# Moving the modulation's first sixteen weight units behind later chunks of w_in, and one bank and the mean's place in na_in

## The chip, the cores and the metric

One core of one Trainium2 chip runs one program. The metric is the device time of one execution in microseconds (us); lower is better. The kernel before takes 1294.21 us, the median of 3 runs (1294.12 to 1294.3).

## What is computed

Two blocks over 256 tokens of width 1024, in float32. The first is an RMS norm, one wide projection w_in (pooling input, q, k, v, index q and k, index weights, gates), pooling and an indexed sparse attention, an output projection, and a convolutional feed-forward. The second is modulated by a vector `ada`, made from two condition vectors and a weight of 2 x 1024 x 6144, and has a mixer, a neighbourhood attention over 16 heads, and feed-forwards. What matters here, cut from the reference:

```
proj = xn @ w_in
score = einsum('bqh,bhqk->bqk', w, relu(einsum('bqhd,bkd->bhqk', iqb, ik) * 64**-0.5))
_, idx = lax.top_k(score, 64)
o = softmax over the chosen keys, times v
...
sx1, cx1, gx1, sx2, cx2, gx2 = split(silu(c) @ ada_w[i] + ada_b[i])
sc1, cc1, gc1, sc2, cc2, gc2 = split(silu(c_ctx) @ ada_w[i] + ada_b[i])
hx = _modulate(_rms(x, g), sx1, cx1)
...
q, k, v = _heads(hx, w_q, q_g), _heads(hx, w_k, k_g), _heads(hx, w_v)   # q and k normed per head
```

## The kernel before, in words

All weights come as **units** of 128 x 1024 float32 (512 KB). `PLAN` (`weight_plan`, line 105) is one list of all units in the order in which they are loaded. SyncE (SP) loads unit i into `raw[i % 9]` (`load`, line 517) as soon as TensorE (PE) is done with unit i - 9; it waits for that in the order of the list, so a ring of nine buffers runs ahead of PE. ScalarE (ACT) makes the high part of a unit, `whi` (L1401, four buffers), and VectorE (DVE) the low part, `wlo`, in place of `raw` (L1917). PE multiplies each 128 x 128 block three times (L634, L646, L648), so a chunk of w_in (one unit, eight blocks) is 24 matmuls of 128 x 256. Which `hi` and `lo` an engine makes at which step is a table of `split_places` (line 153): ACT copies a unit three to four chunks ahead of PE, and waits there for the unit's load (L1399). Each engine takes its instructions in program order, so what stands behind such a copy on ACT waits with it.

w_in's 37 chunks carry other work between them. PE does an index step behind chunks 11 to 18 (`index_heads`, L915; ACT's relu L1464; DVE sums, then finds the largest at L2082 and L2084 behind chunks 16 to 23). Behind chunks 25, 27, 29 and 31 PE makes the attention's scores (`scores1`, L927). DVE masks them and finds the maxima (L2101, L2104), ACT takes the exponential (`exp1`, L1472), DVE the inverses (L2112), GpSimd (POOL) the probabilities (L2729). PE turns those behind chunks 27 to 34 (`turned1`, L936), and ACT copies them out (`copied1`, L1479), which PE waits for before it turns the next head in the same bank and before `values1` (L948) behind chunks 29, 31, 33 and 35. DVE evicts each chunk (`rescaled_in`, L1944).

`ada`'s first sixteen units, called ada 0 to 15, are multiplied on PE (`ada_unit`, L802) into bank 7, in four **runs** of four behind w_in's chunks 9, 13, 17 and 21 (`ADA_AFTER`). DVE copies the bank once, behind the last run (L1951), and PE turns it behind chunk 34. The other 80 units are summed on DVE and are not touched here.

na_in has 24 chunks (`NA_CHUNKS`: k0 q0 v0 k1 q1 k2 ...), a k or v chunk 128 x 512, a q chunk 128 x 256. A chunk's bank is its place in the list of all chunks modulo 3, unless `APART` names one; `bank_free` (line 728) holds PE until the bank is read. For k and q, ACT copies and squares the product (L1841, L1844), PE sums the squares (L1218), DVE takes the mean (`mean_of`, L2503), ACT and POOL make the root, DVE scales (L2509). `scores2` (L1225) uses the same two banks, 4 and 5, in turn with these sums: a use waits until the last but one is read (`na_bank`). Bank 3 is otherwise used by `product2` (L1252) for the values.

Of the kernel before, what the change touches and what calls it, by code (L numbers as in the profile page):

```python
# [46 lines left out]
ADA_STEPS = 96  # L47

LOW_P = range(2)
ADA_AFTER = {"w_in": (6, 16)}  # L50

# [44 lines left out]
             "w_down": "down_r", "ab_in": "ab", "ab_out": "about_r", "w1_0a": "r0a", "w2_0a": "d0a_r",  # L98
             "w1_0b": "r0b", "w2_0b": "d0b_r", "na_in": "na", "na_out": "nao_r", "w1_1": "r1", "w2_1": "d1_r"}

APART = {("w_in", 3): 3, ("w_in", 4): 5, ("w_in", 5): 7, ("pool_w", 1): 5, ("pool_w", 3): 4, ("na_out", 3): 4, ("na_out", 4): 5, ("na_out", 5): 7}
NRAW, NHI = 9, 4


def weight_plan():


    plan, following, order = [], {}, []
    taken, added = [n for n in range(ADA_STEPS) if n not in MOD], MOD[:]

    def modulation(count, places, units):
        for _ in range(count):
            places.append(len(plan))
            plan.append(("ada", units.pop(0)))

    for name in ORDER:
        kt, nt = WEIGHTS[name]
        first, upto = ADA_AFTER.get(name, (0, 0))
        for u in range(-(-kt * nt // 8)):
            order.append(len(plan))  # L120
            plan.append((name, u))
            here = following[name, u] = []
            if u > first and (u - first) % 4 == 3 and upto and taken:
                modulation(4, here, taken)
            modulation(sum(x == u for x in MOD_AFTER.get(name, ())), here, added)
            order += here
    assert not taken and not added and sorted(order) == list(range(len(plan)))
    return plan, following, order


PLAN, FOLLOWING, TAKEN = weight_plan()
TAKEN_AT = {i: e for e, i in enumerate(TAKEN)}
UNIT = {key: i for i, key in enumerate(PLAN)}
# [5 lines left out]
def walk(name):  # L139

    kt, nt = WEIGHTS[name]
    for blk in range(kt * nt):
        if blk % 8 == 0:
            yield "unit", blk // 8
        if blk % kt == kt - 1:
            yield "chunk", blk // kt
        if blk % 8 == 7 or blk == kt * nt - 1:
            yield "after", blk // 8
            for i in FOLLOWING[name, blk // 8]:
                yield "ada", i  # L150
# [124 lines left out]
def bank_left(name, n):  # L275

    if n < EARLY.get(name, 0):
        return "resc_" + name, n + 1
    if name == "ab_in" and n >= 8:
        return "ab_v", n - 7  # L280
    if (name, n) == ("ab_out", 6):
        return "about_r", 15
    twice = name in ("ab_out", "w2_0a", "w2_0b")
    return BANK_READ[name], 2 * n + 2 if twice else n + 1


def launch_program(nc, dram, out):
# [5 lines left out]
    S = Signals(nc)  # L293
# [54 lines left out]
    def param(name, i=0, n=1):  # L348
        at, _ = PARAMS[name]
        return par[:, at + i:at + i + n]  # L350
# [23 lines left out]
    def bank_of(name, n):  # L374
        return ps[APART.get((name, n), CHUNK_AT[name, n] % 3)]

# [56 lines left out]
    def rows_of(h):  # L433
        return slice(64 * (h % 2), 64 * (h % 2) + 64)
# [21 lines left out]
    scores_after = {START2[p] + b: (p, b) for p in range(8) for b in range(2)}  # L456
# [9 lines left out]
    def norm2(n):  # L466

        kind, c = NA_CHUNKS[n] if 0 <= n < 24 else ("v", 0)
        if kind == "v":
            return None  # L470
        return (2 * c, k2[c % 3], 512) if kind == "k" else (2 * c + 1, q2[c % 3], 256)
# [119 lines left out]
    def tensor_program(e):  # L591
        w = Waits(e)
        bank6 = [None]

        def linear(name, T, acts, hi_ready, lo_ready, during=None, following=None, midway=None, begin=0,
# [5 lines left out]
            for n in range(begin, upto or nt):  # L601
                Tn = T(n) if callable(T) else T
                g = CHUNK_AT[name, n]
                bank = bank_of(name, n)
                o = bank[:, :Tn]
                bank_free(name, n)
                for k in range(kt):
                    blk = n * kt + k
# [119 lines left out]
        def bank_free(name, n):  # L728

            if name == "na_out" and n in (3, 4):  # L730
                w.wait_ge(S("na_bank"), len(turn2))
            elif name == "na_out" and n == 5:
                w.wait_ge(S("p2_pt1"), 16)
            elif name == "na_out" and n >= 6:
                w.wait_ge(S("nao_r"), n - 5)
            elif name == "pool_w" and n in (1, 3):
                w.wait_ge(S("sc_x"), 8)
            elif (name, n) == ("w_attn", 0):

                w.wait_ge(S("resc_w_in"), 36)  # L740
            elif name == "w_in" and n < 9:

                if n >= 6:
                    w.wait_ge(S("resc_w_in"), n - 5)
            elif CHUNK_AT[name, n] >= 3:
                signal, count = bank_left(*CHUNKS[CHUNK_AT[name, n] - 3])
                w.wait_ge(S(signal), count)
# [495 lines left out]
        def product2(p):  # L1243

            w.wait_ge(S("p2_pt0"), 2 * p + 2)
            w.wait_ge(S("p2_pt1"), 2 * p + 2)
            w.wait_ge(S("v2"), p + 1)
            if p:
                w.wait_ge(S("o2"), p)
            for k in range(4):  # L1250
                for x in range(2):
                    m = e.matmul(ps[3][rows_of(x), 0:256], v2[p % 3][:, k, rows_of(x)], pts[x][:, 256 * k:256 * k + 256],  # L1252
                                 start=k == 0, stop=k == 3)
            m.then_inc(S("pv2").sem, 1)
# [17 lines left out]
        def after_na(u):  # L1272
            turned, scores, values = attend2(u)
            if values is not None:
                product2(values)
            if turned:
                turned2(*turned)
            if scores:
                scores2(*scores)
# [628 lines left out]
    def vector_program(e):  # L1908
        w = Waits(e)
# [10 lines left out]
        def los(i):  # L1920
            for s in LO_AT[i]:
                lo(s)
# [79 lines left out]
        def written(name, n):  # L2002
            if (name, n) in MOD_SUMMED:
                ada_copied(MOD_SUMMED[name, n])
            if (name, n) in ADA_WRITTEN:
                ada_out(ADA_WRITTEN[name, n])
# [301 lines left out]
        for what, i in walk("ab_in"):  # L2308
            if what == "unit":
                los(UNIT["ab_in", i])  # L2310
            if what == "chunk":
                n, c = i, i % 4
# [133 lines left out]
        for x in "ab":  # L2446
            name, down = "w1_0" + x, "w2_0" + x
# [50 lines left out]
        def head_mean(j, T):  # L2498
            w.wait_ge(S("hn_sum"), j + 1)
            if j >= 2:  # L2500
                w.wait_ge(S("hn_rr"), j - 1)
            bank = ps[4 + turn2["norm", j] % 2]
            e.tensor_scalar(tmp[j % 2][:, :T], bank[:, :T], 1.0 / 64, EPS, MUL, ADD).then_inc(S("na_bank").sem, 1)  # L2503

        def head_out(j, T, dst, gain):
            c, kind = j // 2, j % 2
            w.wait_ge(S("hn_rr"), j + 1)
            w.wait_ge(S("na_copy"), j + 1)
            e.scalar_tensor_tensor(dst, dst, gain, tmp[2 + j % 2][:, :T], MUL, MUL).then_inc(S("hn_out").sem, 1)  # L2509

        def values_out(c):
            w.wait_ge(S("v2_tr"), c + 1)
            if c >= 3:
                w.wait_ge(S("pv2"), c - 2)
            e.tensor_copy(v2[c % 3], ps[6].rearrange("p (t c) -> p t c", t=4)).then_inc(S("v2").sem, 1)
# [36 lines left out]
        def after_na(u):  # L2552
            turned, scores, values = attend2(u)
            if values is not None:
                out2(values)
            if turned:
                turned2(*turned)
            if u == 24:
                lo(SPLIT_AT["na_out", 2])
            if scores:  # L2560
                scores2(*scores)
            if u == 24:
                lo(SPLIT_AT["na_out", 3])

        def values_before(n):

            if n and not norm2(n - 1):
                values_out(NA_CHUNKS[n - 1][1])

        def mean_of(n):  # L2570
            if norm2(n):
                j, _, T = norm2(n)
                head_mean(j, T)

        def during_na(n):

            if n > 4:
                mean_of(n - 1)
            for m in () if n == 2 else (0, 1) if n == 3 else (n - 2,):
                if norm2(m):  # L2580
                    j, dst, T = norm2(m)
                    head_out(j, T, dst, param("q_g" if j % 2 else "k_g"))
            if n < 4:
                mean_of(n - 1)
            written("na_in", n)

        for what, i in walk("na_in"):
            if what == "unit":
                if i not in (3, 4):
                    values_before(i)  # L2590
                if i == 4:
                    mean_of(3)
                if i:
                    los(UNIT["na_in", i])
                if i == 4:
                    values_before(3)
            if what == "chunk":
                during_na(i)
            if what == "after":
                after_na(i)  # L2600
# [18 lines left out]
        for what, i in walk("w1_1"):  # L2619
            if what == "unit":  # L2620
                los(UNIT["w1_1", i])
            if what == "chunk":
                n = i
# [379 lines left out]
```

## Time and profile before

| | |
|---|---|
| median of 3 runs | 1294.21 us |
| the profiled execution's own time | 1294.86 us |
| its span, first to last instruction | 1293.1 us |
| PE busy | 1275.7 us |
| DVE, ACT, POOL busy | 964.6, 594.9, 424.9 us |
| granted TensorE clock, mean | 1.00 |
| read from HBM | 217.21 MB |

The span is all but 1.8 us of the execution's own time. Busy times are sums of the instructions' spans; the ends of matmuls are modelled, so a stall of PE is best seen as the distance between the starts of two matmuls. The page gives the share of the span for each engine; w_in runs from 7 to about 147 us, na_in from 899 to about 1092 us.

### The profile page before, as it was taken

The numbers are of one execution on the slowest core, as the hardware profiler recorded it, in microseconds if no ns is written. First come the engines' busy times: TensorE is split into PE (matmuls) and PEld (weight loads), VectorE is DVE, ScalarE is ACT, GpSimd is POOL, SyncE is SP. The second block draws the span as 40 slices with busy tenths as digits, with TensorE's granted clock in tenths as the row PEclk, the third lists the DMA queues.
The fourth block names the chain that finished last, engine by engine and source line by source line (L and its number), as shares of the span: only waits on it lengthen the run. The fifth ranks groups of instructions, "written<-read, shape, count | busy, mean of one in ns | idle before, by whom it ended". The sixth has DMA issues, their size and how long they took to land.

```text
span 1293.1 us, 19800 instructions
## 1 busy us (share of the span) xinstructions
PE 1275.7 (99%) x7680; PEld 1097.0 (85%) x7680; DVE 964.6 (75%) x1380; ACT 594.9 (46%) x968; POOL 424.9 (33%) x416
## 2 busy tenths in 40 slices
PE   8999999999999999999999999999999999999999
PEld 8888989999888888888788787888767777998887
DVE  6688698999987898897667476566677766977553
ACT  6237556666653233444211243223555554766432
POOL 1562131333330002365200266012466552454100
PEclk9999999999999999999999999999999999999999
DMA  9774466555663553354456365563232332555552
GB/s 306 264 262 157 151 211 199 181 180 186 205 214 112 188 207 126 115 170 159 148 194 194 116 226 210 189 228 127 107 107 73 115 98 70 183 187 186 190 182 79
DMA packets 66268, 219.96 MB, mean 170 GB/s; under 512 B 9120, under 2 KB 12448, under 8 KB 66176
## 3 DMA queue, kind: packets, MB, share of 16 engines
q1 hardware_dynamic: 65888, 218.46, 50.3%
q8 instruction: 61, 1.00, 0.3%
q10 hardware_dynamic: 288, 0.25, 0.1%
q14 instruction: 31, 0.25, 0.1%
HBM read 217.21 MB, written 1.05 MB: 169 GB/s over the span
## 4 chain that ended last, share of the span: by engine, by line
PE 75%; DVE 14%; issue 5%; DMA 2%; ACT 2%; POOL 1%; SPq 0%; DVEq 0%; ACTq 0%; POOLq 0%
PE ps L634 15%; PE ps L648 15%; PE ps L646 15%; PE ps L624 11%; PE ps L626 6%; DVE wlo L1917 4%; DVE tmp L2207 2%; DMA raw<-in_w_in 2%; DVE Y L1944 1%; PE ps L1225 1%; PE ps L1252 1%; PE ps L1239 1%; DVE modsum L1999 1%; PE ps L1218 1%; PE ps L718 1%
## 5 line engine op out<-in xcount | busy, mean ns | idle before, releaser
L1401 ACT ACTIVATE whi<-raw 128x1024 fp32r<-128x1024 f32 (+1 forms) x302 | 317.3, 1052 | 305.5 <-DMA raw<-in_w_0b 73.7
L634 PE MATMUL ps<-A,whi 128*128 128x256 f32 (+2 forms) x1332 | 440.4, 331 | 0.8 <-ACT sq L1844 0.8
L1917 DVE TENSOR_TENSOR wlo<-raw,whi 128x1024 fp32r<-128x1024 f32 (+1 forms) x302 | 400.8, 1332 | 47.7 <-ACT whi L1401 47.7
L648 PE MATMUL ps<-A,wlo 128*128 128x256 f32 (+2 forms) x1312 | 422.9, 322 | 1.7 <-DVE wlo L1917 1.7
L646 PE MATMUL ps<-A,whi 128*128 128x256 f32 (+2 forms) x1312 | 422.4, 322 | 0.2 <-DVE A L1930 0.2
L634 PEld LDWEIGHTS ps<-A,whi 128*128 128x128 f32 x1332 | 253.0, 190 | 41.6 <-issue 18.5
L648 PEld LDWEIGHTS ps<-A,wlo 128*128 128x128 f32 x1312 | 249.2, 190 | 21.8 <-DVE wlo L1917 2.5
L646 PEld LDWEIGHTS ps<-A,whi 128*128 128x128 f32 x1312 | 249.4, 190 | 20.2 <-issue 1.7
L1999 DVE SCALAR_TENSOR_TENSOR modsum<-raw,cond,modsum 128x1024 f32<-128x1024 f32 x98 | 154.4, 1605 | 0.0
L624 PE MATMUL ps<-H,whi 128*128 128x512 f32 x400 | 141.8, 399 | 0.2 <-POOL H L2672 0.2
L2672 POOL TENSOR_TENSOR H<-tmp,H 128x256 fp32r<-128x256 f32 (+1 forms) x86 | 111.9, 1301 | 88.7 <-ACT H L1736 75.1
L626 PE MATMUL ps<-H,wlo 128*128 128x256 f32 x400 | 112.5, 281 | 0.5 <-DVE wlo L1917 0.4
L2808 POOL TENSOR_TENSOR tmp<-tmp 128x512 f32<-128x512 f32 (+1 forms) x42 | 60.7, 1445 | 132.8 <-ACT tmp L1728 132.8
L648 PE MATMUL ps<-H,wlo 128*128 128x512 f32 (+1 forms) x264 | 100.3, 380 | 0.6 <-DVE wlo L1917 0.6
L634 PE MATMUL ps<-H,whi 128*128 128x512 f32 (+1 forms) x264 | 100.4, 380 | 0.0
L646 PE MATMUL ps<-H,whi 128*128 128x512 f32 (+1 forms) x264 | 100.2, 379 | 0.0
L624 PEld LDWEIGHTS ps<-H,whi 128*128 128x128 f32 x400 | 75.2, 188 | 18.9 <-issue 0.5
L2683 POOL TENSOR_TENSOR ssum<-ssum,sq 128x256 f32<-128x256 f32 (+1 forms) x29 | 33.3, 1149 | 161.7 <-ACT sq L1420 161.7
L626 PEld LDWEIGHTS ps<-H,wlo 128*128 128x128 f32 x400 | 75.6, 189 | 1.2 <-DVE wlo L1917 1.2
L624 PE MATMUL ps<-A,whi 128*128 128x512 f32 x182 | 65.2, 394 | 0.0
L2359 DVE SCALAR_TENSOR_TENSOR R<-ps,ada,R 128x256 f32<-128x256 f32 x50 | 22.2, 478 | 52.3 <-PE ps L648 51.8
L648 PEld LDWEIGHTS ps<-H,wlo 128*128 128x128 f32 x264 | 49.7, 188 | 10.1 <-DVE wlo L1917 0.8
(369 smaller groups left out, 1846.5 us busy)
## 6 DMA issues: line engine op xcount, KB each, us to landing
raw<-in_ada SPq DMA_DIRECT2D x96, 512.0 KB, 4.0
raw<-in_w SPq DMA_DIRECT2D x64, 512.0 KB, 3.5
raw<-in_w_up SPq DMA_DIRECT2D x44, 512.0 KB, 3.5
raw<-in_w_in SPq DMA_DIRECT2D x34, 512.0 KB, 5.9
raw<-in_w_0a SPq DMA_DIRECT2D x32, 512.0 KB, 3.8
raw<-in_w_0b SPq DMA_DIRECT2D x32, 512.0 KB, 3.6
raw<-in_na_in SPq DMA_DIRECT2D x24, 512.0 KB, 4.9
raw<-in_w_down SPq DMA_DIRECT2D x22, 512.0 KB, 3.5
```

Source lines behind the costliest of these rows:

```text
L624: e.matmul(bank, w_hi, both(k), start=k == 0, stop=False)
L626: m = e.matmul(o, w_lo, ah, start=False, stop=last)
L634: e.matmul(o, w_hi, ah, start=k == 0, stop=False)
L646: e.matmul(o, w_hi, al, start=False, stop=False)
L648: m = e.matmul(o, w_lo, ah, start=False, stop=last)
L1401: e.activation(whi[s % NHI][:, :cols], raw[i % NRAW][:, :cols], ACT.Copy).then_inc(S("whi").sem, 1)
L1917: e.tensor_tensor(wlo[i % NRAW][:, :cols], raw[i % NRAW][:, :cols], plain(whi[s % NHI][:, :cols]), SUB).then_inc(S("wlo").sem, 1)
L1999: d = e.scalar_tensor_tensor(total, raw[i % NRAW], cond[:, k, v:v + 1], total, MUL, ADD)
L2207: e.scalar_tensor_tensor(x[:, 1:256], o[:, 0:255], param("conv_w", 44 + ch), x[:, 1:256], MUL, ADD).then_inc(own.sem, own.up())
L2672: e.tensor_tensor(into, x, plain(hi), SUB).then_inc(S(done).sem, 1)
L2683: e.tensor_tensor(total, total, x, ADD).then_inc(S(st + "_part").sem, 1)
L2808: e.tensor_tensor(x, x, x, MUL).then_inc(S(st + "_sq").sem, 1)
```

## The change

`ADA_AFTER` now lists the chunks themselves: ada 0 to 3 stand behind chunk 25, ada 4 to 7 behind 27, 8 to 11 behind 29, 12 to 15 behind 31, each run after the attention's steps of that chunk. The plan of loads and the places of `hi` and `lo` follow. In na_in, chunk 3 goes to bank 3 in place of the bank of chunk 0, and waits for the last reader of bank 3 in w2_0b (`d0b_r`); the first `product2` waits for chunk 3's reader. On DVE the mean of chunk i - 1 stands ahead of the `lo` of unit i, not behind it, for nine i (those after a `scores2` step whose chunk i - 1 is a k or q); it stood so for i = 4 before.

```
-ADA_AFTER = {"w_in": (6, 16)}
+ADA_AFTER = {"w_in": (25, 27, 29, 31)}
...
-APART = {..., ("pool_w", 3): 4, ("na_out", 3): 4, ...}
+APART = {..., ("pool_w", 3): 4, ("na_in", 3): 3, ("na_out", 3): 4, ...}
...
-        first, upto = ADA_AFTER.get(name, (0, 0))
...
-            if u > first and (u - first) % 4 == 3 and upto and taken:
+            if u in ADA_AFTER.get(name, ()):
                 modulation(4, here, taken)
...
             if name == "na_out" and n in (3, 4):
                 w.wait_ge(S("na_bank"), len(turn2))
+            elif (name, n) == ("na_in", 3):
+                w.wait_ge(S("d0b_r"), 16)
...
             if p:
                 w.wait_ge(S("o2"), p)
+            else:
+                w.wait_ge(S("na"), 4)
...
+        MEAN_FIRST = [4, *(u + 1 for u in scores_after if 4 < u + 1 < 24)]
...
-            if n > 4:
+            if n > 4 and n not in MEAN_FIRST:
                 mean_of(n - 1)
...
-                if i == 4:
-                    mean_of(3)
+                if i in MEAN_FIRST:
+                    mean_of(i - 1)
                 if i:
                     los(UNIT["na_in", i])
```

SP's queue of loads, at w_in's chunks 26 to 31 before. The tiles raw_49 to raw_57 are the ring's nine buffers, in_w_in a chunk of w_in, in_ada a unit of ada:

```order
L530 DMA raw_55<-in_w_in 128x1024
L530 DMA raw_56<-in_w_in 128x1024
L530 DMA raw_57<-in_w_in 128x1024
L530 DMA raw_49<-in_w_in 128x1024
L530 DMA raw_50<-in_w_in 128x1024
L530 DMA raw_51<-in_w_in 128x1024
```

and now, from ada 4 to chunk 31 (the lines of the file have moved by one; chunks 26 and 27 stand just ahead):

```order
L529 DMA raw_54<-in_ada 128x1024
L529 DMA raw_55<-in_ada 128x1024
L529 DMA raw_56<-in_ada 128x1024
L529 DMA raw_57<-in_ada 128x1024
L529 DMA raw_49<-in_w_in 128x1024
L529 DMA raw_50<-in_w_in 128x1024
L529 DMA raw_51<-in_ada 128x1024
L529 DMA raw_52<-in_ada 128x1024
L529 DMA raw_53<-in_ada 128x1024
L529 DMA raw_54<-in_ada 128x1024
L529 DMA raw_55<-in_w_in 128x1024
L529 DMA raw_56<-in_w_in 128x1024
```

Each pair of chunks now has four units of ada ahead of it. The load of chunk 28 (raw_49) is the ring's ninth behind ada 1, that of chunk 29 behind ada 2, and those of chunks 30 and 31 behind ada 5 and 6.

ACT, from the copy of chunk 29 to the copy-out of the first turned head, before (whi_68 to whi_70 are copies of units; the ACT_TABLE_LOAD and the X tiles are the exponential; Y_102 is the copy-out):

```order
L1401 ACTIVATE whi_68<-raw_49 128x1024
L1472 ACT_TABLE_LOAD
L1472 ACTIVATE X_98,small<-X_98,small 128x128
L1472 ACTIVATE X_98,small<-X_98,small 128x256
L1472 ACTIVATE X_99,small<-X_99,small 128x128
L1472 ACTIVATE X_99,small<-X_99,small 128x256
L1527 ACTIVATE sig<-tmp_89 128x256
L1401 ACTIVATE whi_69<-raw_50 128x1024
L1527 ACTIVATE sig<-tmp_90 128x256
L1401 ACTIVATE whi_70<-raw_51 128x1024
L1479 ACTIVATE Y_102<-ps 128x384
```

and now, from the copy of chunk 28:

```order
L1404 ACTIVATE whi_67<-raw_49 128x1024
L1404 ACTIVATE whi_68<-raw_50 128x1024
L1475 ACT_TABLE_LOAD
L1475 ACTIVATE X_98,small<-X_98,small 128x128
L1475 ACTIVATE X_98,small<-X_98,small 128x256
L1475 ACTIVATE X_99,small<-X_99,small 128x128
L1475 ACTIVATE X_99,small<-X_99,small 128x256
L1530 ACTIVATE sig<-tmp_89 128x256
L1530 ACTIVATE sig<-tmp_90 128x256
L1404 ACTIVATE whi_69<-raw_55 128x1024
L1404 ACTIVATE whi_70<-raw_56 128x1024
L1482 ACTIVATE Y_102<-ps 128x384
```

As before, the copies of chunks 28 and 29 stand ahead of the first exponential, and those of 30 and 31 ahead of the first copy-out; what has moved is their place by a step or so, and the buffers that they read, which are those of the loads above. Chunks 32 and 33 stand in the same way ahead of the third head's copy-out.

DVE in na_in, at the step of unit 5, before (wlo_63 is the low part of a later unit, tmp_88 the mean for q1, k_1_145 a scaled k):

```order
L2531 TENSOR_REDUCE small<-X_99 128x1
L2536 RECIPROCAL small<-small 128x1 x2
L1917 TENSOR_TENSOR wlo_63<-raw_54,whi_70 128x1024
L2503 TENSOR_SCALAR tmp_88<-ps 128x256
L2509 SCALAR_TENSOR_TENSOR k_1_145<-k_1_145,par,tmp_89 128x512
```

and now:

```order
L2534 TENSOR_REDUCE small<-X_99 128x1
L2539 RECIPROCAL small<-small 128x1 x2
L2506 TENSOR_SCALAR tmp_88<-ps 128x256
L1920 TENSOR_TENSOR wlo_63<-raw_54,whi_70 128x1024
L2512 SCALAR_TENSOR_TENSOR k_1_145<-k_1_145,par,tmp_89 128x512
```

The mean has changed places with one low part; the other eight places read alike.

## Rows read from the trace of the kernel before

**Rows 1.** page, busy time of each engine over the span

```profile
PE 1275.7 (99%) x7680; PEld 1097.0 (85%) x7680; DVE 964.6 (75%) x1380; ACT 594.9 (46%) x968; POOL 424.9 (33%) x416
```

**Rows 2.** who PE waited for: us in total, times, longest us

```profile
PE ps L915 <- ACT tmp L1464: 1.8, 2, 1.2
...
PE ps L936 <- POOL Y L2729: 0.9, 1, 0.9
...
PE ps L634 <- ACT sq L1844: 0.8, 1, 0.8
...
PE ps L1225 <- DVE tmp L2503: 0.6, 1, 0.6
```

**Rows 3.** timeline of PE in w_in: start us, us, instruction, idle before and releaser

```profile
39.22 1.92 PE L802 MATMUL ps<-raw,cond 128*32 128x512 f32 x16
...
51.79 0.56 PE L915 MATMUL ps<-ik,iq 64*128 64x128 f32 x4 [1.24 <-ACT tmp L1464]
...
103.81 0.38 PE L634 MATMUL ps<-A,whi 128*128 128x256 f32 x1
...
110.81 0.55 PE L936 MATMUL ps<-con,Y 128*128 128x128 f32 x3 [0.93 <-POOL Y L2729]
...
128.94 0.39 PE L634 MATMUL ps<-A,whi 128*128 128x256 f32 x1
```

**Rows 4.** timeline of SP's DMA issues in w_in, around the first modulation run

```profile
40.31 1.28 SPq L530 DMA_DIRECT2D raw<-in_ada  x3
41.63 0.43 SPq L530 DMA_DIRECT2D raw<-in_w_in  x1
```

**Rows 5.** raw tiles' landing, issued in 40:41.4, 56:58.1, 73.2:75.8, 107:112

```profile
DMA to landing us min/median/max: 4.9/6.3/7.5
...
DMA to landing us min/median/max: 5.7/6.6/8.0
...
DMA to landing us min/median/max: 4.4/5.3/6.1
...
DMA to landing us min/median/max: 3.3/3.4/3.5
```

**Rows 6.** DMA issues by line in 41.5:42: count, KB each, median us to landing

```profile
raw<-in_w_in SPq DMA_DIRECT2D x1, 512.0 KB, 8.8
```

**Rows 7.** timeline of ACT in w_in

```profile
50.42 1.06 ACT L1401 ACTIVATE whi<-raw 128x1024 fp32r<-128x1024 f32 x1 [8.80 <-DMA raw<-in_w_in]
...
106.20 1.04 ACT L1401 ACTIVATE whi<-raw 128x1024 fp32r<-128x1024 f32 x1
107.26 1.28 ACT L1472 ACT_TABLE_LOAD   x1
```

**Rows 8.** timeline of DVE in w_in

```profile
68.43 1.23 DVE L1917 TENSOR_TENSOR wlo<-raw,whi 128x1024 fp32r<-128x1024 f32 x1 [2.75 <-ACT whi L1401]
69.58 0.41 DVE L1944 TENSOR_TENSOR vT<-ps,rst 128x256 f32<-128x256 f32 x1
...
94.96 0.68 DVE L1951 COPY tmp<-ps 128x512 f32<-128x512 f32 x1
...
96.69 0.42 DVE L1944 TENSOR_TENSOR tmp<-ps,rst 128x256 f32<-128x256 f32 x1
```

**Rows 9.** 80 to 96 us: length, PE, PEld, DVE, ACT, POOL (instructions), PEclk, DMA, GB/s

```profile
80.00:96.00 16.00, 16.00 (x135) 14.43 (x134) 15.27 (x39) 4.88 (x7) 14.64 (x20) 1.00 0.78 271
```

**Rows 10.** timeline of PE at the start of na_in

```profile
915.83 0.50 PE L634 MATMUL ps<-A,whi 128*128 128x512 f32 x1 [0.82 <-ACT sq L1844]
...
937.60 1.12 PE L1225 MATMUL ps<-k,q 64*128 64x512 f32 x2
...
939.31 0.69 PE L1225 MATMUL ps<-k,q 64*128 64x512 f32 x1 [0.59 <-DVE tmp L2503]
```

**Rows 11.** timeline of DVE at the start of na_in

```profile
937.15 1.77 DVE L1917 TENSOR_TENSOR wlo<-raw,whi 128x1024 fp32r<-128x1024 f32 x1
938.85 0.41 DVE L2503 TENSOR_SCALAR tmp<-ps 128x256 f32<-128x256 f32 x1
```

More of the change, by code:

```diff
@@ L99 @@
              "w1_0b": "r0b", "w2_0b": "d0b_r", "na_in": "na", "na_out": "nao_r", "w1_1": "r1", "w2_1": "d1_r"}
-APART = {("w_in", 3): 3, ("w_in", 4): 5, ("w_in", 5): 7, ("pool_w", 1): 5, ("pool_w", 3): 4, ("na_out", 3): 4, ("na_out", 4): 5, ("na_out", 5): 7}
+APART = {("w_in", 3): 3, ("w_in", 4): 5, ("w_in", 5): 7, ("pool_w", 1): 5, ("pool_w", 3): 4, ("na_in", 3): 3, ("na_out", 3): 4, ("na_out", 4): 5, ("na_out", 5): 7}
 NRAW, NHI = 9, 4
```

## The prediction, made before the changed kernel ran

> **What bounds the kernel now.** First the page's busy times: PE is busy for 1275.7 of 1293.1 us [rows 1], so what remains to gain are stalls of a microsecond or less, and any wait that is added to PE shows in full. Then the list of who PE waited for: in w_in it is ACT's relu (1.8 us in two stalls) and POOL's probabilities (0.9 us), in na_in the square that frees a bank (0.8 us) and the mean that frees bank 4 or 5 (0.6 us) [rows 2]. The timelines show what stands behind these. In w_in ACT sat idle for 8.80 us until 50.42, waiting for the load of chunk 14, and the relu that PE needed stood behind that copy [rows 7]; PE stalled for 1.24 us [rows 3]. The reader should see in this that a late load does not stop PE by itself. It stops ACT's queue, and PE meets it at the next thing that it needs from ACT. From 68.43 DVE does not pause until chunk 26 [rows 8]; it is 95% busy from 80 to 96 us, while PE still runs 135 matmuls in 16 us [rows 9], 0.12 us each or 2.9 us a chunk.
>
> **How loads land around a run.** This carries the forecast. A run of four units takes PE 1.9 us [rows 3]. As it frees four raw buffers, SP issues four loads, at 1.1, 1.5, 2.0 and 2.4 us after the run's start at 39.22 (40.31 to 41.63) [rows 4]. They landed 4.9, 6.3, 7.5 and 8.8 us after issue [rows 5, 6], so the third is there 9.5 us after the run's start, and the fourth 11.2. Reckoned alike with the medians and maxima of the two later bursts [rows 5], the third came at 10.0 and 8.1 us. A load alone takes 3.4 us [rows 5]. The moved runs make the same bursts. What differs is who waits. Before, the fourth load of a burst was chunk 14, copied by ACT some three chunks later. Now chunks 28 and 29 are the second and third loads of the first run's burst, 30 and 31 those of the second's, 32 and 33 those of the third's, and ACT's copies of them stand ahead of the exponential, and then ahead of the copy-out, that PE needs one or two chunks after the run. I take 9.3 us for the third load where one was issued just before the run, and 8.7 to 9 where not.
>
> **Step 1, chunks 9 to 25.** The four runs leave this stretch (7.5 us of PE), and with them the lateness of loads: chunk i's load now waits for chunk i - 9, which is 26 us of work ahead. Chunk 9 ends at 39.1 as before. Chunks 10 to 16 then take 7 x 2.9 and five index steps of about 0.5 [rows 3], to 62.3 us. DVE's unbroken stretch begins there: it evicts chunk 16 at 62.5 in place of 69.58 [rows 8]. The work between that and chunk 22's eviction is unchanged, but for the copy of bank 7 (0.6 us) [rows 8], so that comes at 89.0 in place of 96.69. PE loses most of its lead here, as it can start a chunk only when DVE has reached the eviction two chunks before (the low part stands just ahead of it): I count 2.1, 0.9, 0.5 and 0.5 us of waits for `wlo` at chunks 22 to 25. Chunk 25 ends at 95.0, scores take 0.9, and the first run ends at 97.9. Chunk 26 starts at 97.9 in place of 103.81 [rows 3]: **5.9 us earlier**, with three runs still to come. Bounds: 4 if DVE's steps are stretched by POOL in the new alignment, 7.5 if not at all limited by DVE.
>
> **Step 2, the three later runs: 3 x 1.9 = 5.6 us** on PE. Their own loads were issued long before, so nothing is added there.
>
> **Step 3, new waits of PE.** First run, start 96.0: chunk 29 lands at 105.3, its copy ends at 106.3. From the end of that copy (107.24) to the first turned head it took 3.6 us before, through table load, exponential, inverses and probabilities [rows 3, 7]; so PE can turn at 109.9. It is there after chunk 27, at 103.7: a stall of 6.2 us, where it was 1.0 before. Second run, start 111.2: chunk 31 lands at 119.9, copied at 121.0, the copy-out behind it takes 0.5; PE wants to turn the next head behind chunk 28 at 116.1: 5.4 us. Third run, start 126.9: chunk 33 at 135.9, copy, one more copy of 0.3, copy-out, 137.6; PE is there at 131.8: 5.8 us. Behind chunk 31 the copy of chunk 34 (the fourth load) costs 0.5 more. Sum 17.9, less the 1.0 of before: **+16.9**. The fourth run does no harm: the loads that it frees are for later stages. The queue behind the waiting copy holds all of ACT's work, and DVE's inverses and the evictions behind them; they get late by the same amount, and nothing of this is added to PE's stall. Bounds for the three stalls: with every load landing in 3.4 us they are 2.3, 2.1 and 2.4; with the third as late as the latest fourth (11.6) they are 8.5, 8.3 and 8.4.
>
> So w_in: -5.9 + 5.6 + 16.9 = +16.6 us. Behind it the engines wait for each other as before, PE most of all, and no load is near its limit, so I let the delay through to the end.
>
> **Step 4, na_in.** Chunk 3 no longer waits for chunk 0's square: -0.8 us [rows 10]. What is late next is the chain from the sum behind chunk 3's first half to the scores, which PE starts itself and which moves with it, so I keep the whole 0.8. The mean at unit 5: DVE made the low part from 937.15 to 938.92 and then the mean, PE's second scores matmul came at 939.31 where it could have followed the first of 937.60 after 0.5 [rows 10, 11]. With the mean first that wait is covered: -1.2. The low part is 0.4 later and has two chunks of lead. The other eight swaps have no wait of PE against them: nothing. **-2.0**, bounds -0.5 (both waits reappear at the next step) and -2.5.
>
> **Sum.** +16.6 - 2.0 = +14.6 on the profiled execution's 1294.86, so 1309.5; the median of the runs lies 0.65 lower, which gives 1308.8. I say 1308.5 us.
>
> **A rule against the change.** The granted clock is at its upper level, 2.4 GHz, in the row of 80 to 96 us [rows 9], and so it is in every other stretch; no wait of PE before is above 1.3 us, so no row shows what happens behind one of 5 or 6. The Trainium skill (TensorE: Matmul & The Clock Gate, The HAM clock gate) says that an idle PE falls back to 1.2 GHz and is given 2.4 again only when it has been busy; by it the new stalls would cost up to a chunk's 2.9 us again each, and the sum would be up to 1317. On loads the skill (DMA: Bandwidth & Descriptors, Anatomy of one DMA) puts a transfer at some 2.0 us and its bytes at 436 GB/s, 3.2 us for one load, near the 3.4 measured; its estimate for a third load in a row is 5.6 us, where the trace has 7.5, and by it the sum would be some 6 us lower. I go by the trace.
>
> **Rivals.**
> 1. The loads come quicker than in the three bursts, since the new ones are issued while PE's stalls leave DMA idle. The stalls are then between 2.2 and 4.5 us each, and the time is 1298 to 1304. For it: the third burst before was quicker by 1.4 us than the first. Against: a burst's third load is behind two others issued 0.45 us apart, whatever stands before.
> 2. PE comes back slower from each stall: 1313 to 1318. For it: three idle gaps far longer than any now. Against: part of a slower chunk 28 or 30 would be hidden in the next stall.
> 3. The other side: chunks 28 to 33 are in time, and only the gains stay. Then w_in gives -5.9 + 5.6 - 1.0 = -1.3, with na_in 1291. It decides at the landing: the third load would have to be there 3.3 us after the run's start, or have its buffer from another unit. It is issued 2.0 us after the start and takes 3.3 us at the least [rows 5], so only a fault in my reading of the ring brings this.
> 4. The two edits in na_in do nothing, because the waits move to the next step: 1310.5.
>
> **How the numbers follow.** The forecast and its neighbours within 4 us, rival 4 among them, 0.54; rival 1 0.18; rival 2 0.19; rival 3 0.07, and 0.02 for a time near that of before by a mixture. Left out on the two sides are the slowest part of rival 2 and the quickest of rival 1, beside rival 3: the range is 1299 to 1317. A measurement of this kernel can tell about 0.2% (2.6 us) from no change: faster 0.07, within 0.02, slower 0.91.
>
> **What would show it.** ACT should wait for in_w_in loads three times, ending near 105, 120 and 136, for 5 us and more. PE should wait at L936's successor for POOL's probabilities once (6 us) and for ACT's copy-out twice (5 to 6 us each). No wait of ACT for w_in between 36 and 95, no stall of PE at L915, some at L648 for `wlo` near 80 to 92. The first chunk behind the run at 96 should start near 98, the one behind the fourth near 145. In na_in chunk 3 should follow without a gap, and the mean stand right behind the inverses at unit 5. I am wrong if ACT's longest wait for a load in w_in is below 3 us, if PE has no stall above 3 us there, or if the clock falls.

## The result, and the profile after

The changed kernel takes 1313.09 us, the median of 4 runs (1311.96 to 1314.29); the kernel before, beside it, took 1294.26. The ratio is 1.0146, with an interval of 1.0134 to 1.0158. The forecast was 1308.5 with a range of 1299 to 1317. The profiled execution took 1311.96 us, its span is 1310.1.

The page's busy times after, against [rows 1]:

```profile
PE 1280.8 (98%) x7680; PEld 1101.6 (84%) x7680; DVE 969.9 (74%) x1380; ACT 594.7 (45%) x968; POOL 418.3 (32%) x416
```

The same 7680 matmuls keep PE busy 5.1 us longer. So the 17.0 us of span are not all waiting: some matmuls have become slower. Who PE waited for, against [rows 2] (us in total, times, longest):

```profile
PE ps L937 <- ACT Y L1482: 8.3, 2, 4.3
PE ps L647 <- DVE wlo L1920: 4.8, 7, 1.7
PE ps L937 <- POOL Y L2734: 4.8, 1, 4.8
```

The three stalls of the forecast are there, one for POOL and two for ACT's copy-out. The waits for the index steps, for the square that freed a bank and for the mean are gone from this view. The timeline of PE in w_in, against [rows 3]:

```profile
96.49 1.92 PE L803 MATMUL ps<-raw,cond 128*32 128x512 f32 x16
98.34 0.38 PE L633 MATMUL ps<-A,whi 128*128 128x256 f32 x1
...
109.14 0.90 PE L937 MATMUL ps<-con,Y 128*128 128x128 f32 x3 [4.79 <-POOL Y L2734]
...
121.45 0.87 PE L937 MATMUL ps<-con,Y 128*128 128x128 f32 x3 [4.03 <-ACT Y L1482]
...
122.34 0.41 PE L645 MATMUL ps<-A,whi 128*128 128x256 f32 x1
122.55 0.41 PE L647 MATMUL ps<-A,wlo 128*128 128x256 f32 x1
122.76 0.41 PE L633 MATMUL ps<-A,whi 128*128 128x256 f32 x1
...
138.66 0.88 PE L937 MATMUL ps<-con,Y 128*128 128x128 f32 x3 [4.30 <-ACT Y L1482]
...
148.39 0.38 PE L633 MATMUL ps<-A,whi 128*128 128x256 f32 x1
```

Chunk 26 starts at 98.34, 5.47 us earlier than before, and chunk 32 at 148.39, 19.45 us later. Behind 121.45 matmuls of 128x256 stand 0.21 us apart, where it was 0.12. ACT's timeline says what the stalls are made of:

```profile
103.26 1.06 ACT L1404 ACTIVATE whi<-raw 128x1024 fp32r<-128x1024 f32 x1 [5.42 <-DMA raw<-in_w_in]
104.52 1.06 ACT L1404 ACTIVATE whi<-raw 128x1024 fp32r<-128x1024 f32 x1 [0.21 <-DMA raw<-in_w_in]
105.60 1.28 ACT L1475 ACT_TABLE_LOAD   x1
...
118.60 1.06 ACT L1404 ACTIVATE whi<-raw 128x1024 fp32r<-128x1024 f32 x1 [8.53 <-DMA raw<-in_w_in]
...
135.57 1.06 ACT L1404 ACTIVATE whi<-raw 128x1024 fp32r<-128x1024 f32 x1 [7.27 <-DMA raw<-in_w_in]
```

Three waits for loads of w_in, of 5.4, 8.5 and 7.3 us, each with a second copy 1.2 us behind it. From the end of the second copy at 105.58 to the first turned head at 109.14 it takes 3.56 us, as it did before (3.6). The windows give the clock (length, then PE, PEld, DVE, ACT, POOL, then PEclk, DMA share, GB/s):

```profile
105.00:106.00 1.00, 0.00 (x0) 0.00 (x0) 0.57 (x1) 0.98 (x2) 0.00 (x0) 1.00 1.04 397
106.00:107.00 1.00, 0.00 (x0) 0.00 (x0) 0.00 (x0) 0.99 (x2) 0.00 (x0) 0.78 1.01 365
107.00:108.00 1.00, 0.00 (x0) 0.00 (x0) 0.09 (x1) 1.00 (x5) 0.00 (x0) 0.50 0.40 160
112.00:113.00 1.00, 1.00 (x8) 0.20 (x4) 0.96 (x4) 0.00 (x0) 0.00 (x0) 0.50 0.00 0
113.00:114.00 1.00, 1.00 (x12) 0.19 (x4) 0.97 (x4) 0.00 (x0) 0.00 (x0) 0.81 0.00 0
114.00:115.00 1.00, 1.00 (x10) 0.71 (x7) 1.00 (x1) 0.00 (x0) 0.00 (x0) 1.00 0.51 123
```

PE stops at 104.3. The granted clock goes from 2.4 to 1.2 GHz at about 106.5, while PE is idle; PE works again from 109.14, and the clock is back shortly after 113. The same happens behind the other two stalls. That agrees with the rule of the Trainium skill cited in the prediction (TensorE: Matmul & The Clock Gate, The HAM clock gate). No stretch of the kernel before could show it: its longest wait of PE is 1.24 us.

In na_in the timeline of PE, against [rows 10]:

```profile
955.60 1.13 PE L1226 MATMUL ps<-k,q 64*128 64x512 f32 x4
958.85 1.10 PE L1219 MATMUL ps<-sq,con 128*128 128x512 f32 x2 [0.49 <-DVE X L2532]
```

The four scores matmuls run in one piece. A new wait of 0.49 us for DVE has come behind them, at the next sum of squares. The two kernels lie 19.07 us apart just ahead of na_in (the norm's matmuls there start at 896.38 and 915.45), 18.00 at the first sum of squares (918.69 and 936.69) and 17.04 at the first matmul behind the sum at 958.85 (942.34 and 959.38): the edits gave 2.03 us.

### The profile page after: what moved, and what is told of

Same layout as the page of the kernel before. It is cut to its first block, busy times and chain, and to the rows that moved or that the text cites. A ratio compares the mean times of both kernels' runs of the same rounds, so it can differ in the third digit from the quotient of the medians.

```text
span 1310.1 us, 19800 instructions
## 1 busy us (share of the span) xinstructions
PE 1280.8 (98%) x7680; PEld 1101.6 (84%) x7680; DVE 969.9 (74%) x1380; ACT 594.7 (45%) x968; POOL 418.3 (32%) x416
## 4 chain that ended last, share of the span: by engine, by line
PE 75%; DVE 15%; issue 5%; ACT 2%; DMA 2%; POOL 1%; SPq 0%; DVEq 0%; ACTq 0%; POOLq 0%
PE ps L633 15%; PE ps L647 15%; PE ps L645 15%; PE ps L623 11%; PE ps L625 5%; DVE wlo L1920 5%; DVE tmp L2210 2%; DMA raw<-in_w_in 2%; DVE Y L1947 1%; PE ps L1255 1%; PE ps L1226 1%; PE ps L1240 1%; DVE modsum L2002 1%; DVE score L2069 1%; PE ps L803 1%
```

## The experiments

The theory after this reading: a run of four frees its buffers late, the load of a chunk then lands behind the time at which ACT wants to copy it, and what PE needs stands in ACT's queue behind that copy. The fall of the clock comes on top. Rivals: the loads themselves bind PE, whatever ACT's order; the slow matmuls have another cause than the clock; a part of the loss is na_in's.

### na_in alone

Both edits, then the bank alone, then the mean alone, each on the kernel before with its own `ADA_AFTER`.

```
-APART = {..., ("pool_w", 3): 4, ("na_out", 3): 4, ...}
+APART = {..., ("pool_w", 3): 4, ("na_in", 3): 3, ("na_out", 3): 4, ...}
...
+        MEAN_FIRST = [4, *(u + 1 for u in scores_after if 4 < u + 1 < 24)]
...
-                if i == 4:
-                    mean_of(3)
+                if i in MEAN_FIRST:
+                    mean_of(i - 1)
```

> The kernel before with the two edits in na_in alone; the four runs stay behind chunks 9, 13, 17 and 21. My theory: the two edits are worth 2.0 us and nothing of the loss is theirs, so 1292.3 us. Rival: the waits only move to the next step, or depend on the later arrival of na_in in the changed kernel; then 1293.8 to 1294.3.

> The kernel before with na_in's chunk 3 in bank 3 alone. The prediction gave this edit 0.8 us; the trace of the changed kernel has the first sum of squares 1.1 us nearer to the start of na_in than before. So 1293.1 to 1293.5 us. Rival: chunk 3 is quicker, but the scores behind it wait for DVE as long as before: 1294.2.

> The kernel before with the mean ahead of the low part at nine units of na_in, chunk 3's bank as before. The prediction gave it 1.2 us: 1293.0 us. What the trace of the changed kernel leaves for it beside the bank is 0.9 us net: 1293.3. The two edits together should be worth their sum within 0.4 us; if each alone were worth nearly the whole 2.0, they would be two ways out of one wait.

Measured: both 1292.4 us, ratio 0.9988 (0.998 to 0.9996); the bank 1293.8, 0.9995 (0.9986 to 1.0004); the mean 1293.98, 1.0 (0.999 to 1.001), beside 1294.14. So the pair is a gain, and either alone is below what these runs can tell; both medians lie above what I had expected of them, by 0.3 and 0.7 us. The spans of the profiled executions are 1290.7, 1292.1 and 1292.3, against 1293.1. PE's timeline, first with the bank, then with the mean alone, shows each:

```profile
910.82 4.26 PE L1288 MATMUL ps<-A,whi 128*128 128x512 f32 x21
917.68 1.02 PE L1220 MATMUL ps<-sq,con 128*128 128x512 f32 x2
```

```profile
937.76 1.13 PE L1225 MATMUL ps<-k,q 64*128 64x512 f32 x4
941.00 1.10 PE L1218 MATMUL ps<-sq,con 128*128 128x512 f32 x2 [0.48 <-DVE X L2529]
```

With the bank the first sum of squares stands at 917.68, and at 918.69 without, from starts that lie 0.07 us apart: 1.08 us. With the mean it is 3.24 us from the scores to the sum, of which 0.48 are the new wait, and 3.77 to the matmuls behind it; before 4.74 from [rows 10] to 942.34: 0.97 us. The two add up to the 2.0 of both, and nothing of the loss is here.

### Matmuls in the stalls

```
+FILLER = {27: 36, 28: 32, 30: 34}
+        def filler(u, count):
+            bank_free("w_in", u + 1)
+            for _ in range(count):
+                e.matmul(bank_of("w_in", u + 1)[:, :256], E_hi[:, 0, 0:128], E_hi[:, 1], start=True, stop=True)
...
+            if u in FILLER:
+                filler(u, FILLER[u])
             if u in TURNED:
                 turned1(TURNED[u])
```

> The changed kernel with matmuls of 128x256 put in ahead of the three waits before the turned heads behind chunks 27, 28 and 30: 36, 32 and 34 of them, 0.12 us each, 4.3, 3.8 and 4.1 us, into the bank of the next chunk, which is free there. They are shorter than the stalls of 4.8, 4.3 and 4.6 us and compute nothing that is used. My theory, in two parts: the stalls are waits for ACT and stay as long (each head is turned at the same distance from the run before it), and the slow matmuls behind them (0.21 us in place of 0.12) are the granted clock's fall alone. Then the granted clock stays at 1.00 and the time falls by 5 to 6.5 us: 1306.5 to 1308 us. Rival: the matmuls behind the stalls are slow because their operands come late; then the time stays at 1313.

Measured: 1308.83 us (1307.48 to 1309.24), ratio to the kernel before 1.0109 (1.0094 to 1.0124), 4.3 us under the changed kernel. The windows of this run and, below them, those of the changed kernel:

```profile
110.00:115.00 5.00, 5.00 (x42) 3.07 (x43) 3.85 (x9) 0.75 (x2) 0.73 (x2) 1.00 0.27 83
125.00:130.00 5.00, 5.00 (x44) 2.75 (x45) 3.25 (x8) 0.42 (x1) 0.00 (x0) 1.00 0.44 134
```

```profile
110.00:115.00 5.00, 5.00 (x31) 2.20 (x31) 3.28 (x7) 0.07 (x1) 0.00 (x0) 0.66 0.11 26
125.00:130.00 5.00, 5.00 (x39) 3.73 (x42) 0.94 (x2) 0.42 (x1) 0.00 (x0) 0.80 0.35 99
```

With nothing but useless work in the gaps the clock stays at 1.00, and the real matmuls behind them stand 0.12 us apart again. The slow matmuls were the clock's. The gain is less than the 5 to 6.5 us expected, as the waits for the heads are longer: from the last real matmul to the turned head 5.7, 5.4 and 4.6 us, where it was 5.0, 4.2 and 4.5, and the values behind chunk 31 wait 0.9. PE comes to chunk 28's end at 116.15 in place of 117.27, but the copy that it needs then does not come earlier. A part of the slow clock had been hidden in the next stall. The first head is late for another reason, at 109.99 in place of 109.14: SP's two issues of chunks 28 and 29 took 1.64 us here and 0.91 in the changed kernel, and ACT's copy of chunk 29 started at 105.37 in place of 104.52. I have no cause for the slower issue.

### ACT's order

```
+COPIES_BEHIND = (26, 28, 30, 32)
...
+                late = list(HI_AT[UNIT["w_in", i]]) if i in COPIES_BEHIND else []
...
                 if i - 1 in SCORES:
                     exp1(SCORES[i - 1])
+                for s in held + late:
+                    hi(s)
+                held = []
             if what == "ada":
-                his(i)
+                held += HI_AT[i]
...
                     out1_lo(VALUES[i - 1])
+                for s in LO_AT[UNIT["w_in", i]] if i in COPIES_BEHIND else ():
+                    lo(s)
```

> The changed kernel, its loads, runs and buffers as they are, with ACT's copies of chunks 28 and 29, 30 and 31, 32 and 33, and 35 behind the exponential and copy-outs of their step, and DVE's low parts of 28, 30, 32 and 34 behind the inverses. My theory: a late load hurts only through what stands behind its copy in ACT's queue. Then the heads are turned without a long stall, and chunk 28 is copied at 104 to 105 us, before PE wants it: 1291.5 to 1296 us, with no fall of the clock. Rival: the loads themselves are the bound (six to eight of them in a row at 380 to 400 GB/s), and PE then waits for the high or low parts of chunks 28 to 33 instead: 1304 us or more.

Measured: 1299.99 us (1297.62 to 1300.88), ratio 1.004 (1.0025 to 1.0055): 13.1 us won by the order of ACT's copies and DVE's low parts alone, with every load, run and buffer where it was in the program, but 4 us more than the theory's range. PE's largest wait, and ACT's timeline ahead of it:

```profile
PE ps L950 <- ACT Y L1483: 5.2, 2, 2.8
```

```profile
113.03 1.06 ACT L1405 ACTIVATE whi<-raw 128x1024 fp32r<-128x1024 f32 x1 [3.17 <-DMA raw<-in_w_in]
114.39 1.06 ACT L1405 ACTIVATE whi<-raw 128x1024 fp32r<-128x1024 f32 x1 [0.30 <-DMA raw<-in_w_in]
115.71 0.42 ACT L1536 ACTIVATE sig<-tmp 128x256 f32<-128x256 f32 x1 [0.26 <-DVE tmp L1953]
116.03 0.47 ACT L1483 ACTIVATE Y<-ps 128x384 f32<-128x384 f32 x1
```

I had moved the copies behind the first copy-out, and so ahead of the second, for which the values wait. The same queue, one step later; the clock fell behind these stalls too. So the copies of chunks 30 to 33 were put behind the second copy-out as well:

```
+HELD, FLUSHED = (26, 28, 29, 30, 31), (26, 29, 31)
+                held += late
+                if i not in HELD or i in FLUSHED:
+                    for s in held:
+                        hi(s)
```

> The changed kernel as in the run with the copies behind the exponential, but the copies of chunks 30 to 33 (and DVE's low parts of 30 and 32) also behind the second copy-out, one step later. The two stalls that were left there, 2.8 and 2.4 us before the values behind chunks 29 and 31, were waits for a copy-out that stood behind the copies of chunks 30 and 31, 32 and 33. My theory: they go, and the clock's fall behind them: 1292 to 1294.5 us. Rival: the loads are too late for PE itself once ACT's queue is out of the way; PE waits for whi or wlo at chunk 30 or 32: 1297 or more.

Measured: 1291.54 us (1291.24 to 1291.87), ratio 0.9968 (0.9957 to 0.9979). PE waits for no head and no value any more, but for the 0.4 us that it waits for DVE's `ada` ahead of one head in the kernel before too. ACT's copies of chunks 28 and 29 in this run:

```profile
103.80 1.06 ACT L1405 ACTIVATE whi<-raw 128x1024 fp32r<-128x1024 f32 x1 [2.48 <-DMA raw<-in_w_in]
105.06 1.06 ACT L1405 ACTIVATE whi<-raw 128x1024 fp32r<-128x1024 f32 x1 [0.20 <-DMA raw<-in_w_in]
```

They come 0.5 us later than in the changed kernel, and cost nothing: PE wants chunk 28 at 107.61. Chunk 32 starts at 128.11, where it was 128.94 before and 148.39 in the changed kernel. With these loads the late place of the runs is no slower than the early one with the na_in edits (1292.4). So the rival that the loads themselves bind PE is out, and all of the loss in w_in was what stood behind the copies, and the clock that fell with it. The low parts on DVE were moved together with the copies, and no run moves one of the two alone.

### The size of the other loads, and runs of two

```
+            if name == "ada" and u < 16 and i >= NRAW:
+                e.dma_start(raw[i % NRAW][:, :16], dram[name][u][:, :16]).then_inc(S(f"load{i % NRAW}").sem, 16)
+                return
```

> The changed kernel with the loads of ada 0 to 15 cut from 512 KB to 16 columns (8 KB), and the matmuls of the four runs reading another tile of the same shape and type: the modulation's first sixteen units are left out of the computation. Order, buffers and issues stay. My theory: the third load of a burst then lands some 4 to 5 us after its issue in place of 6 to 7, the three stalls shrink to 2 to 3 us each (my lower bounds were 2.3, 2.1 and 2.4), the clock falls little or not: 1299 to 1303 us. Rival, the other loads in the burst are no matter, only the issue is late: 1310 or more. If the other loads are all of it, and the copies come in time: 1292 to 1295.

Measured: 1308.36 us (1306.8 to 1310.01), ratio 1.0108 (1.0093 to 1.0123), 4.7 us under the changed kernel, well above the range and nearer to the rival's 1310. PE's stalls are 4.4, 2.7 and 3.3 us, where the same view has 4.8, 4.0 and 4.3 for the changed kernel, and the clock falls behind all three. The first hardly shrinks: ACT's copies start at 102.98 and 104.25 in place of 103.26 and 104.52. In this run SP's two issues took longer:

```profile
98.02 2.10 SPq L532 DMA_DIRECT2D raw<-in_w_in  x2
```

against 0.91 us in the changed kernel. Chunk 29 landed 4.5 us after its issue in place of 6.1, but was issued later, which hides what the first burst would have gained. The same two issues took 1.64 us in the run with matmuls in the stalls and 1.96 in the first one with ACT's order changed, so this is not the short loads' doing; I have no cause for it. The other two stalls give 1.3 and 1.0 us. So what ada's loads take from those of w_in is at most a third of a stall; the greater part is that the load is only issued when its buffer is free, 1.5 to 2 us after the run's start (2.3 to 2.8 where the run itself goes at the slow clock), and then takes its own time.

```
-ADA_AFTER = {"w_in": (25, 27, 29, 31)}
+ADA_AFTER = {"w_in": range(25, 33)}
...
-                modulation(4, here, taken)
+                modulation(2, here, taken)
```

> The changed kernel with two units of ada behind each of the chunks 25 to 32 in place of four behind 25, 27, 29 and 31: as late in w_in, the same number of loads, but two buffers freed at a time. My theory: each load waits behind one other in place of three, but the mean rate asked of the DMA queues is the same; stalls of 1 to 2 us each in place of 4.5, too short for the clock to fall: 1297 to 1304 us. Rival: only the rate counts, and it is at its limit from 98 to 140 us: 1309 or more.

Measured: 1301.06 us (1300.21 to 1302.32), ratio 1.0051 (1.0035 to 1.0068). Two stalls are left, 2.2 and 3.0 us, rather than many of 1 to 2, and the clock, which I had expected to hold, falls behind both: it is at 0.50, 1.2 GHz, from 113 to 115 and from 133 to 136. Half the burst takes out more than half of the loss, with the same bytes.

### Earlier, and finer

```
-ADA_AFTER = {"w_in": (25, 27, 29, 31)}
+ADA_AFTER = {"w_in": range(9, 25)}
...
-                modulation(4, here, taken)
+                modulation(1, here, taken)
```

> Both na_in edits, and the sixteen units of ada one at a time, behind each of the chunks 9 to 24, in place of four runs of four. My theory: lateness comes from four buffers freed within 2 us; one at a time frees one buffer for each 3.4 us of PE's work, so no load of w_in comes late, ACT's idle time of 8.8 us at chunk 14's load goes, and with it the stalls of PE at the index steps (1.8 us): 1290.5 us, 1289.5 to 1291.5. Rival: these stalls come from the order of relu and copies on ACT and not from the loads: then as with the na_in edits alone, 1292.3.

Measured: 1297.32 us (1296.86 to 1298.31), ratio 1.0025 (1.0016 to 1.0033), where I had expected 1290.5. The stalls at the index steps are gone, as foreseen; what I had not priced is PE's own time. PE's timeline of one unit here, and of a pair in the run with late pairs:

```profile
43.03 1.05 PE L803 MATMUL ps<-raw,cond 128*32 128x512 f32 x4
44.02 0.38 PE L633 MATMUL ps<-A,whi 128*128 128x256 f32 x1
```

```profile
100.72 1.07 PE L803 MATMUL ps<-raw,cond 128*32 128x512 f32 x8
101.72 0.38 PE L633 MATMUL ps<-A,whi 128*128 128x256 f32 x1
```

One unit takes 0.99 us to the next chunk's first matmul, two take 1.00, four took 1.85 [rows 3]. Sixteen single units cost 15.8 us where four runs cost 7.4: 8.4 more, of which 4.9 show beside the run with the na_in edits, so 3.5 us of stalls were won. PE's waits up to the end of w_in agree: they sum to 5.5 us in that run and to 2.1 here. Pairs keep that gain and lose little:

```
-ADA_AFTER = {"w_in": range(9, 25)}
+ADA_AFTER = {"w_in": range(9, 24, 2)}
...
-                modulation(1, here, taken)
+                modulation(2, here, taken)
```

> Both na_in edits, and ada's units in pairs behind the chunks 9, 11, 13 to 23. In the run with single units a unit alone took PE 0.98 us, a run of four 1.85, and in the run with late pairs a pair 0.99: a pair costs what a single unit costs. My theory: eight pairs cost 0.5 us more than four runs of four (7.9 against 7.4), bursts of two loads are as harmless as single ones, and the 3.3 us of stalls that single units took away go here too: 1289.6 us. Rival: a burst of two still makes a load late for ACT at the index steps, or DVE's unbroken work from 60 to 96 us takes the gain back: 1292 to 1293.

Measured: 1289.81 us (1289.72 to 1290.37), ratio 0.9956 (0.9944 to 0.9969). This is faster than both kernels, by 0.44% against the kernel before and by some 23 us against the change. What is left of PE's waits for low parts and for heads, over the whole kernel (in w_in the first is 1.0 us in two waits):

```profile
PE ps L647 <- DVE wlo L1920: 1.7, 3, 0.6
...
PE ps L937 <- POOL Y L2734: 0.7, 1, 0.7
```

Last, whether the stalls at the index steps of the kernel before are the same mechanism:

```
+RELU_FIRST = (11, 12, 13, 14)
+            if what == "after" and i in INDEX_MM:
+                index_relu(INDEX_MM[i])
+                for s in HI_AT[UNIT["w_in", i]] if i in RELU_FIRST else ():
+                    hi(s)
```

> Both na_in edits, the four runs at 9, 13, 17 and 21, and at the steps of chunks 11 to 14 ACT's copies behind the relu in place of ahead of it. My theory: the two stalls at the index steps (1.8 us) are the queue behind the late copy of chunk 14, and go; but DVE bounds PE from 80 to 96 us, and its unbroken work there begins with the low part of a chunk whose load is late as before, so a part of the gain is taken back: 1290.6 to 1292 us. Rival: the stalls stay (relu is late for its own reason): 1292.4.

Measured: 1291.14 us (1290.84 to 1292.08), ratio 0.9969 (0.9957 to 0.998), 1.3 under the run with the na_in edits. The two were not run side by side (the kernel before took 1295.28 beside this one and 1294.14 beside the other), so the traces have to settle it. The run with the na_in edits has the wait

```profile
PE ps L917 <- ACT tmp L1468: 1.2, 1, 1.2
```

and this one none at the index steps, with 2.6 us of waits for low parts in both. From the first index step to the scores behind chunk 25 PE takes 55.78 us there (46.76 to 102.54) and 54.28 here (46.92 to 101.20). So the stall at the second index step was the queue behind chunk 14's copy, and its 1.2 us came back whole; nothing was taken back by DVE, as I had thought it would be. The other stall of the kernel before (0.6 us) is not in the run with the na_in edits either, and these runs do not say why.

## Why the prediction was right, and where not

**Step 1** held. Chunk 16's eviction came at 62.42 (62.5 foreseen), chunk 22's at 89.37 (89.0), the first run at 96.49 (96.0), chunk 26 at 98.34 (97.9). The terms written for chunks 10 to 16 give 61.9 and not 62.3, so the nearness of the first of these owes something to rounding. Waits for `wlo` in w_in were 4.2 us over six (4.8 over seven in the whole kernel), 3.1 of them at chunks 22 to 25, where I had 4.0. **Step 2** held: the last two later runs take 1.86 us each, and the second more only through the clock.

**Step 3** had the mechanism, the three places, the engines waited for and what stands in the queue; the two runs with ACT's order changed show that it is this queue. Its size was off. I took the third load's landing as 9.3 and 8.7 to 9 us after the run's start. By the start of its copy on ACT it came 8.0, 8.3 and 7.4 us after (104.52 - 96.49, 119.88 - 111.55, 136.81 - 129.38). So the stalls, between matmuls, are 5.0, 4.2 and 4.5 us where I had 6.2, 5.4 and 5.8, in all 12.7 more than before in place of 16.9. Third in the row of issues (97.58, 97.95, 98.4), chunk 29 landed 6.1 us after its issue; I had gone by 7.5 from the first burst before. The third burst before has 6.1 for its third load, the second 8.0 [rows 5], so the trace of the kernel before held the right figure among three and did not say which to take. The Trainium skill (DMA: Bandwidth & Descriptors, Anatomy of one DMA) gives 2.0 us and 436 GB/s for one transfer, in a section on loads that GpSimd issues, where these are SP's; it has no figure for loads in a row. The 5.6 us for a third load is an estimate worked out from these two (2.0 and three times 1.2), and it was nearer here than 7.5.

**The clock** was left out of the sum and named as rival 2, at 0.19. It came true on top of the forecast's mechanism, and the prediction itself says that it is wrong there if the clock falls. What it cost: from the turned head to the next chunk or run PE took 5.15, 7.93 and 7.87 us, and 3.14, 5.42 and 5.43 in the run without stalls: 7.0 us. From chunk 26's start to chunk 32's it is 50.05 us in the changed kernel and 29.48 in that run; the difference of 20.6 is the stalls, 13.6, and the clock, 7.0. With the filler only some 4 of the 7 came back, as rival 2's own counter-argument had it. The failed step is thus the line that kept the clock out since no row showed it; a stall of 5 us that is forecast is itself a reason to forecast the fall. Four us too much of stall and seven of clock left out gave +19.1 at the start of na_in, where I had 16.6. These two errors have opposite signs, and that the forecast of 1308.5 came within 4.6 us is in part luck: with the stalls as they were and the clock still left out it would have been some 1304, 9 us too low.

**Step 4.** The sum of 2.0 was right to 0.1, the parts less: the bank 1.1 in place of 0.8, the mean 1.0 in place of 1.2, since the wait for the mean gave back 0.5 as a new wait at the next sum of squares.

**Sum.** For the profiled execution 1309.5 was forecast and 1311.96 measured; the other runs of the changed kernel are longer, so the median lies 1.1 above it, not 0.65 below.

**Rivals.** Rival 1 had part of the truth, the quicker loads: two of the three stalls, 4.2 and 4.5 us, lie in its range, though not its time, since the clock came on top. Rival 2 had the rest, and the median lies at the lower end of its 1313 to 1318. Rival 3, that only the gains stay, did not come for this kernel. I had given it to a fault in my reading of the ring alone, at 1291; with the copies behind the second copy-out a changed order reaches that time, 1291.54, with the loads as late as before. Rival 4, the na_in edits worth nothing, is refuted by the trace and by the run with both (ratio 0.998 to 0.9996).

## What to carry to other kernels

Before a group of loads is moved, look on the engine that consumes them for what stands behind each consumer in its queue; put the work that others wait for ahead of a copy that may be late, and the late load cost nothing here. When a forecast contains a stall of PE, add to it the slower matmuls behind it: here 2.0 to 2.5 us behind each stall of 4.2 to 5.0, some 1.6 behind one of 2.8 or 3.0, nothing behind 1.24 or 1.71, less what the next stall hides. Free buffers in small steps, but price the steps on PE itself: here two units side by side cost what one does.

## What had not been expected of the hardware

A single unit of ada takes PE 0.99 us and two take 1.00, eight matmuls of 128*32 by 512 in the trace in place of four. In the program the second unit of a pair writes the other 64 of the bank's partitions; that the two run beside each other is my reading, and no run isolates it.

In the changed kernel the granted clock fell 2.2 us after PE had stopped at 104.3, and PE worked some 4 us at 1.2 GHz before it was back. In the first run with ACT's order changed, a stall of only 2.8 us (113.8 to 116.56) brought the fall too, and later than the stall itself: PE had been at work for 1.1 us when the clock fell, at about 117.7, and it stayed at 1.2 GHz until 121. The windows there:

```profile
116.00:117.00 1.00, 0.44 (x4) 0.34 (x6) 0.01 (x1) 0.81 (x3) 0.00 (x0) 1.00 0.78 320
117.00:118.00 1.00, 1.00 (x11) 0.52 (x7) 0.00 (x0) 0.38 (x1) 0.00 (x0) 0.83 0.34 123
118.00:119.00 1.00, 1.00 (x9) 0.87 (x8) 0.00 (x0) 0.49 (x1) 0.00 (x0) 0.50 0.00 0
```

From the values at 116.56 to the next chunk PE took 5.56 us, and 3.99 in the second run with ACT's order changed, which has no stall there: the slow clock cost 1.6 us on top of the 2.8. The shortest stall with a fall is the one of 2.2 us in the run with late pairs; there the clock fell at about 112.4, just after PE was back:

```profile
112.28 0.80 PE L937 MATMUL ps<-con,Y 128*128 128x128 f32 x3 [2.18 <-ACT Y L1482]
```

```profile
112.00:113.00 1.00, 0.72 (x3) 0.43 (x3) 0.00 (x0) 1.00 (x6) 0.00 (x0) 0.69 1.02 389
113.00:114.00 1.00, 1.00 (x9) 0.20 (x8) 0.25 (x3) 0.88 (x5) 0.70 (x2) 0.50 0.38 152
```

Behind that run's stall of 3.0 us PE took 4.70 us from the values to the next chunk, where it takes 3.14 without a stall: again some 1.6. The stall of 1.24 us before [rows 3] cost nothing more, nor did the one of 1.71 us for a low part at 82.03 in the changed kernel: the windows from 79 to 86 have the clock at 1.00.

In the changed kernel the loads of chunks 28 and 29, issued 0.4 us apart (97.95 and 98.4), landed 5.3 and 6.1 us after their issue, some 1.2 us apart. With ada's loads cut to 8 KB those of chunks 30 and 31, issued some 0.5 us apart from 113.61 on, landed 3.5 and 4.2 us after, again some 1.2 us apart.
